# A transformer layer step on one core: halved border tiles leave PSUM by halves, the fourth tile starts on half of the tokens, and the last sums of squares stand behind three operands

## The reference, cut to what matters

```
h  = x + 0.5 * rmsnorm(swiglu(rmsnorm(x, g1), Wg, Wu, Wd), g1post)        # feed-forward 1
p  = rmsnorm(h, gmix) @ W_in         # gates and forget gate, fox q k v, nsa q k v
o  = concat(rmsnorm(fox_attention(p)), rmsnorm(nsa_attention(p)))
h2 = h + rmsnorm(o @ W_out, gmixpost)
y  = h2 + 0.5 * rmsnorm(swiglu(rmsnorm(h2, g2), Wg2, Wu2, Wd2), g2post)    # feed-forward 2
```

## Time and profile before

| | |
|---|---|
| median of three runs | 1217.18 us (1216.4 to 1220.91) |
| time of the profiled execution | 1218.23 us |
| its span | 1216.1 us |
| TensorE busy, share of the span | 96% |
| VectorE, ScalarE, GpSimd | 45%, 35%, 12% |
| mean granted TensorE clock | 0.983 |
| DMA | 117.53 MB, mean 97 GB/s |
| border a | about 400 to 441 us from the span's start |
| border b | about 805 to 845 us |

### The profile page before, as it was taken

One profiled execution on the slowest core, in us unless ns is written; L12 is line 12 of the kernel. 1 busy time (PEld: TensorE's weight loads), 2 busy tenths in 40 slices (PEclk: granted clock), 3 DMA queues, 4 the chain that ended last, 5 costly groups with the idle time before them and its releaser, 6 DMA issues.

```text
span 1216.1 us, 23337 instructions
## 1 busy us (share of the span) xinstructions
PE 1165.3 (96%) x9450; PEld 1076.8 (89%) x9460; DVE 542.6 (45%) x845; ACT 426.5 (35%) x779; POOL 146.4 (12%) x151
## 2 busy tenths in 40 slices
PE   8999999999999989998998899989999999999996
PEld 6999999999999889996545556978999999999995
DVE  3443333334333844354545767584333323343335
ACT  5322221222234642223523546464222212232332
POOL 0101100001012000131301312200011000010110
PEclk9999999999999999998998999999999999999998
DMA  6313222322123124224754310311232233232232
GB/s 277 105 69 103 81 85 83 113 92 103 58 87 120 50 90 157 88 70 120 162 144 143 105 70 2 121 53 63 77 103 81 68 102 100 101 104 69 67 105 73
DMA packets 50321, 117.53 MB, mean 97 GB/s; under 512 B 8347, under 2 KB 27163, under 8 KB 44579
## 3 DMA queue, kind: packets, MB, share of 16 engines
q1 hardware_dynamic: 48210, 112.68, 28.3%
q10 hardware_dynamic: 2032, 3.74, 0.8%
HBM read 107.79 MB, written 7.97 MB: 95 GB/s over the span
## 4 chain that ended last, share of the span: by engine, by line
PE 89%; DVE 5%; issue 3%; ACT 2%; DMA 1%; SPq 0%; DVEq 0%; ACTq 0%
PE ps L1627 69%; PE ps L1673 4%; PE ps L2123 3%; PE ps L1827 2%; PE ps L1860 2%; PE ps L1844 2%; PE ps L1894 1%; DVE row_max L1295 1%; DVE PTS L534 1%; DVE Y L1119 1%; PE ps L1636 1%; PE ps L1701 1%; DMA RAW<-in_w_gu 1%; PE ps L1835 1%; PE ps L1790 1%
## 5 line engine op out<-in xcount | busy, mean ns | idle before, releaser
L1627 PE MATMUL ps<-XH,WH 128*128 128x260 f32 x1680 | 342.3, 285 | 8.4 <-DVE XL L1081 3.3
L463 ACT CAST WH<-RAW 128x1024 fp32r<-128x1024 f32 (+2 forms) x177 | 168.7, 953 | 509.4 <-PE ps L1627 496.8
L1627 PE MATMUL ps<-XH,WL 128*128 128x260 f32 x1680 | 339.6, 284 | 0.0
L1627 PE MATMUL ps<-XL,WH 128*128 128x260 f32 x1680 | 339.1, 284 | 0.0
L1627 PEld LDWEIGHTS ps<-XH,WH 128*128 128x128 f32 x1680 | 261.0, 189 | 10.9 <-issue 8.3
L466 DVE TENSOR_TENSOR WL<-RAW,WH 128x1024 fp32r<-128x1024 f32 (+2 forms) x177 | 196.5, 1110 | 153.4 <-ACT WH L463 152.1
L1627 PEld LDWEIGHTS ps<-XH,WL 128*128 128x128 f32 x1680 | 260.2, 189 | 0.0
L1627 PEld LDWEIGHTS ps<-XL,WH 128*128 128x128 f32 x1680 | 259.5, 189 | 0.0
L1532 POOL TENSOR_TENSOR UL<-HT,UH 128x520 f32 (+1 forms) x44 | 57.7, 1311 | 634.1 <-ACT UH L813 634.1
L1627 PE MATMUL ps<-UL,WH 128*128 128x260 f32 x664 | 133.8, 283 | 0.0
L1627 PE MATMUL ps<-UH,WL 128*128 128x260 f32 x664 | 133.5, 282 | 0.0
(11 more groups left out here) (292 smaller groups left out, 1291.0 us busy)
## 6 DMA issues: line engine op xcount, KB each, us to landing
RAW<-in_w_gu SPq DMA_DIRECT2D x43, 1024.0 KB, 4.8
RAW<-in_w_down SPq DMA_DIRECT2D x16, 768.0 KB, 4.6
RAW<-in_w_down SPq DMA_DIRECT2D x16, 640.0 KB, 4.3
RAW<-in_w_in SPq DMA_DIRECT2D x10, 1024.0 KB, 4.9
KF<-in_fox_k SPq DMA_DIRECT2D x16, 256.0 KB, 4.2
VF<-in_fox_v SPq DMA_DIRECT2D x16, 256.0 KB, 4.0
RAW<-in_w_out SPq DMA_DIRECT2D x4, 1024.0 KB, 5.6
H<-in_x SPq DMA_DIRECT2D x4, 520.0 KB, 7.8
```

The lines of the kernel that those rows point to most:

```text
L463: nc.scalar.copy(hi[:, 0:width], RAW[:, slot, j, 0:width]).then_inc(w_hi, 1)
L1627: q = nc.tensor.matmul(ps[:, 2 * slot + half, 0:HALF], w[:, par, cols], x[:, kt0 + kt, half * HALF:(half + 1) * HALF], start=first and kt ...
```

## The change

1. `half_sums(s, 1)` (for a and b) moves from ahead of the warm-up into `border_products`, behind the third operand of half 0. TensorE waits for all three early items behind the warm-up.
2. VectorE copies each of the three tiles out in two halves: half 0 after half 0's 1/rms (`halves_out`), half 1 after half 1's. `first_halves` counts the three tiles whose half 0 is complete.
3. TensorE does the fourth item in two halves (`fourth_half`): half 0 straight behind the border, in bank 2, whose content is then copied out already; half 1 after the second half of that tile is out. At a the transposes of the first tile stand between them.
4. ScalarE's and VectorE's split of the fourth item, and ScalarE's scale of half 0, move from amid the operands to behind them. At a, the split of the fifth item moves there too, from `project`.
5. The logarithm of these scales is written into another buffer (`SQ`).
6. `softplus` loads one table set that has both its functions.

```diff
                 e = 1 if factor == 4 else 0
-                nc.scalar.activation(ST[:, 0, columns(h)], ps[:, 4 + h, 0:HALF], ACT.Ln, scale=factor / D_MODEL,
+                log = (SQ if kind == "hss" else ST)[:, 0, columns(h)]
+                nc.scalar.activation(log, ps[:, 4 + h, 0:HALF], ACT.Ln, scale=factor / D_MODEL,
                                      bias=const("eps")[:, e:e + 1]).then_inc(sem(kind + "_ln"), 1)
                 act.wait_ge(sem(kind + "_ln"), since(kind + "_ln", s, h + 1))
-                nc.scalar.activation(dst[:, columns(h)], ST[:, 0, columns(h)], ACT.Exp, scale=-0.5).then_inc(
-                    sem(done), 1)
+                nc.scalar.activation(dst[:, columns(h)], log, ACT.Exp, scale=-0.5).then_inc(sem(done), 1)
...
                             half_rstd(s, 1, "yss", factor, GT[:, 0, :], "yrstd")
-                        elif h == 1 and t == 3:
-                            split(first + 3)
-                        elif h == 1 and t == 5:
-                            half_rstd(s, 0, "hss", 1, R1[:, :], "rstd")
+                split(first + 3)
+                half_rstd(s, 0, "hss", 1, R1[:, :], "rstd")
                 half_rstd(s, 1, "hss", 1, R1[:, :], "rstd")
+                if s == "a":
+                    split(first + 4)
...
+                nc.scalar.preload_act_table_set("natural_log_exp_and_others")
                 act.wait_ge(sem("lf_abs"), 1)
...
                 for j in range(NPROJ):
-                    if 2 <= j < NPROJ - 2:
+                    if 2 < j < NPROJ - 2:
                         split(IT_PROJ + j + 2)
...
                                                            op1=ALU.subtract).then_inc(sem("xlo"), 1)
-                        if h == 1 and t == 7 and name:
-                            split(first + 3)
                     if name:
...
                         nc.vector.tensor_tensor(Y[:, 4, c], Y[:, 4, c], Y[:, 5, c], ALU.add).then_inc(sem("hacc"), 1)
-                if name:
-                    dve.wait_ge(sem("rstd"), since("rstd", s, 2))
+                if not name:
+                    return
+                out = [TR[:, 0, :], TR[:, 1, :], TR[:, 2, :]] if s == "a" else [GT[:, 0, :], UT[:, 0, :], GT[:, 1, :]]
+                dve.wait_ge(sem("first_halves"), 3 if s == "a" else 6)
+                dve.wait_ge(sem("rstd"), since("rstd", s, 1))
+                for n in (1, 0, 2):
+                    nc.vector.tensor_tensor(out[n][:, columns(0)], ps[:, 2 * (0, 1, 3)[n], 0:HALF], R1[:, columns(0)],
+                                            ALU.mult).then_inc(sem("halves_out"), 1)
+                    if n == 1:
+                        split(first + 3)
+                dve.wait_ge(sem("rstd"), since("rstd", s, 2))
+                for n in range(3):
+                    dve.wait_ge(used, first + n + 1)
+                    nc.vector.tensor_tensor(out[n][:, columns(1)], ps[:, 2 * (0, 1, 3)[n] + 1, 0:HALF],
+                                            R1[:, columns(1)], ALU.mult).then_inc(sem("projected" if s == "a" else "evac"), 1)
+                if s == "a":
+                    split(first + 4)
...
                     if st.kind == "gu":
-                        dve.wait_ge(used, k + 1)
-                        nc.vector.tensor_tensor(two(GT[:, st.par, :]), halves(3 if f == 1 and st.number == 1 and st.g == 0
-                                                                              else 0), two(R1[:, :]),
-                                                ALU.mult).then_inc(sem("evac"), 1)
+                        known = st.number if f == 1 and st.g == 0 else None
+                        if known not in (0, 1):
+                            dve.wait_ge(used, k + 1)
+                            nc.vector.tensor_tensor(two(GT[:, st.par, :]), halves(0), two(R1[:, :]),
+                                                    ALU.mult).then_inc(sem("evac"), 1)
                         split_behind(f, st, 0)
-                        dve.wait_ge(used, k + 2)
-                        nc.vector.tensor_tensor(two(UT[:, st.par, :]), halves(1), two(R1[:, :]),
-                                                ALU.mult).then_inc(sem("evac"), 1)
+                        if known != 0:
+                            dve.wait_ge(used, k + 2)
+                            nc.vector.tensor_tensor(two(UT[:, st.par, :]), halves(1), two(R1[:, :]),
+                                                    ALU.mult).then_inc(sem("evac"), 1)
                         split_behind(f, st, 1)
...
                 for j in range(NPROJ + 1):
-                    if j < NPROJ:
+                    if 3 <= j < NPROJ:
                         dve.wait_ge(used, IT_PROJ + j + 1)
...
                                 dve.wait_ge(sem("turned_out"), 1)
-                        nc.vector.tensor_tensor(two(TR[:, j % 4, :]), halves(3 if j == 2 else j % 2), two(R1[:, :]),
+                        nc.vector.tensor_tensor(two(TR[:, j % 4, :]), halves(j % 2), two(R1[:, :]),
                                                 ALU.mult).then_inc(sem("projected"), 1)
-                    if j == 2:
-                        split(IT_PROJ + j + 2)
                     if j > 0 and TILES[j - 1] in ROPED:
...
-                for n in range(2):
-                    ready(first + n)
                 if s == "a":
...
                 keep_warm(WARM[1], 0)
-                ready(first + 2)
+                for n in range(3):
+                    ready(first + n)
                 for h in (0, 1):
...
                             q = part(n, kt, h)
-                            if h == 1 and kt == KT - 1:
+                            if h == 0 and kt == KT - 1:
+                                q.then_inc(sem("first_halves"), 1)
+                            elif kt == KT - 1:
                                 q.then_inc(used, 1)
+                        if h == 0 and kt == 2:
+                            half_sums(s, 1)
                         if kt >= KT - HSQ_PE:
...
+            def fourth_half(k, h):
+
+                par = k % 2
+                for kt in range(KT):
+                    q = half_product(WH[:, par, :], WL[:, par, :], kt, True, kt, 2 + h, h, kt == 0, kt == KT - 1)
+                if h == 1:
+                    q.then_inc(used, 1)
+
             def half_token_squares(s, h):
...
                         ready(k + 1)
+                        pe.wait_ge(sem("halves_out"), 4)
+                        fourth_half(k + 1, 0)
                         pe.wait_ge(sem("evac"), since("evac", f, st.M * 2))
-                        products((IT_F[f] + 1) % 2, KT, XH, XL, 1)
+                        fourth_half(k + 1, 1)
                         return
...
                                 q.then_inc(sem("half_done"), 1)
-                        half_sums(s, 1)
+                        if s == "c":
+                            half_sums(s, 1)
                         return
...
                 border_products("a", IT_PROJ)
+                ready(IT_PROJ + 3)
+                pe.wait_ge(sem("halves_out"), 1)
+                fourth_half(IT_PROJ + 3, 0)
+                turn(0)
                 pe.wait_ge(sem("projected"), 2)
-                turn(0)
-                for j in range(3, NPROJ):
+                fourth_half(IT_PROJ + 3, 1)
+                for j in (1, 2):
+                    pe.wait_ge(sem("projected"), j + 1)
+                    turn(j)
+                for j in range(4, NPROJ):
                     ready(IT_PROJ + j)
...
                     products((IT_PROJ + j) % 2, KT, XH, XL, j % 2)
-                    if j == 3:
-                        pe.wait_ge(sem("projected"), 3)
-                        turn(1)
                     turn(j - 1)
...
             q.then_inc(used, 1)
-            half_sums("b", 1)
             ffn(1, "b", "c")
```

## The result

The changed kernel takes 1200.09 us (median of 4 runs, 1198.45 to 1202.06) against 1216.83 us for the kernel before (1216.4 to 1220.91); the ratio is 0.9856 with a 95% interval of 0.983 to 0.9882, that is 16.7 us or 1.4% faster. The prediction said 1200.0 us in a range of 1197.0 to 1204.5. The profiled execution took 1198.45 us, 1196.5 of it the span.

What follows compares the result with a forecast made beforehand. TensorE, busy 96% of the span, was taken as the bound, losing time to stops and half clock at borders. Gains of 11.0 (a) and 6.75 (b) sum to 17.75 us; from median 1217.18, with 0.6 held back: 1200.0 us, range 1197.0 to 1204.5.

Steps and rivals of the forecast that it cites:

- Start of the border: At both borders, tiles start just behind the first operand, no longer after the last sums: 402.85 at a, 808.72 at b.
- Length of the border, S minus the start of the tiles: From first tile to S, the border's last matmul pair of squares: about 22.2 us at both borders.
- The fourth tile and the fifth item at a: Behind border a, half the fourth tile replaces 2.49 us idle; the fifth item starts at 431.8, 9.3 us earlier.
- The clock: At border a, TensorE's idle times go and full clock is kept: 1.74 us more, 11.0 in all there.
- The sixth weight: Behind border a: cast at 434.5, done at 436.9, wanted by TensorE at 437.6; margin 0.7 us, no cost.
- Border b: Fifth item starts 6.75 us earlier, 1.77 of it clock, despite a new 1.1 us stall for its weight.
- 0.6 held back for handovers: In the forecast total: 0.6 us kept back for handovers taken as free, making 1199.4 into 1200.0 us.
- A new stretch of half clock in the borders: Rival, chance 0.11: new idle times at b bring half clock; one stretch costs 1.75 us: 1201.8, two 1203.5.
- ScalarE is not the bound at a: Rival, chance 0.06: table loads cost twice 1.28 us, sixth weight 1.9 late, stall at b 1.3 longer: 1203.2.
- The overlap works: Rival, chance 0.04: first-half copies come behind the border, the fourth tile waits; 2.5 us back at each border, 1205.
- The gain is not lost further on: Rival, chance 0.05: the attention stage, with stops of its own, loses part of the gain: 1206 to 1213 us.
- The projections did not stay at half clock: Rival, chance 0.02: TensorE, started earlier, stays at 1.2 GHz through the projections: 1229 us.

Runs made afterwards that it cites:

- same: The changed kernel run again with no edit, to see its noise: 1200.10 us, ratio 0.9862 to the kernel before.
- sums_first: Changed kernel with the last sums of squares put back ahead of the warm-up: 1206.81 us, ratio 0.9931 to the kernel before.
- three_tables: Changed kernel without the explicit table load in softplus, so three loads at border a in place of two: 1201.15 us, one run.
- no_warm: Changed kernel without the 8 warm-up matmuls ahead of each border: 1200.90 us, ratio 0.9872 to the kernel before.
- whole_fourth: Changed kernel, but TensorE begins the fourth item only when both halves of the first two tiles are out: 1202.54 us, ratio 0.9902 to before.
- only_sums: Kernel before with only the last sums of squares moved behind three operands: 1208.08 us, ratio 0.9930 to the kernel before.
- same_again: The changed kernel unaltered once more, in a later series: 1199.73 us, ratio 0.9875 to the kernel before.

## Why the prediction was right

*Start of the border.* The tiles were forecast to begin 0.54 us behind the start of the first operand's low part (402.85 and 808.72 on the time line of before); they begin 0.63 us behind it at both borders (403.04 - 402.41 at a).

*Length of the border, S minus the start of the tiles.* Predicted 22.25 and 22.2; measured 22.19 (425.23 - 403.04) and, in `same`, within 0.02 of it at both borders. The sums cost the 0.8 us that was forecast: without them, in `sums_first`, it is 21.4.

*The fourth tile and the fifth item at a.* Predicted at S + 6.7, measured 6.78. The gain up to the fifth item was forecast as 9.3 and is 9.18, counted from the first operand: 441.09 - 402.31 before, 432.01 - 402.41 after.

*The clock.* 1.74 us more at a: the part of the ledger has 10.89 for a forecast of 11.0. The prediction priced the half clock behind two stops alone. The falls in the warm-ups of before stood unnamed in the 5.2 us (4.2 at b) from first operand to tiles that lie in its rows, so the sum has them all the same. The granted clock is 1.00 throughout both borders, in this trace and in the two of the same kernel.

*The sixth weight.* The cast was forecast at 434.5 and starts at 434.48; it is done in time. `three_tables` shows how thin the margin is: one load more and the weight is 0.47 us late.

*Border b.* The fifth item was forecast with a stall of 1.1 us at S + 7.3 and has 1.27, at S + 7.65 (824.07 - 816.42 in `same`, whose records are complete there). VectorE's low part takes 1.43 us again, as in the earlier trace rows, where I had put the usual 1.23. So the gain to that item is 6.3 and not 6.75; the part of the ledger has 6.0, and where the other 0.3 went is open. The parts sum to 10.9 + 6.0 = 16.9 where 17.75 was forecast; the 0.6 held back for handovers happened to cover most of it. That the forecast met the median to 0.1 us is luck: the gain between medians was 16.7, 15.7 and 15.2 us in three series, and the forecast took 17.2 off a median of before that was itself 0.35 us higher than that of the final four runs.

*The rivals.* A new stretch of half clock in the borders did not come, and `no_warm` and `whole_fourth` show that it can at longer idle times (3.5 us, and 1.9 us against the 1.76 us that stayed without effect). The argument that both new idle times were shorter than any followed by a fall was too narrow, though: in the trace of before, 1.55 us of idle time ahead of a transpose at 562.62 has half clock behind it from 564.4 on. ScalarE is not the bound at a. The overlap works. The gain is not lost further on: the attention stage varies by 3 us by itself. The projections did not stay at half clock.

What the prediction missed was outside of the change: before's profiled execution had 2.7 us in the attention stage that after's did not have. Starting from the median of before and not from that execution took 1.05 us of it off; how much of it the median of before holds, no trace shows.

The order of the parts by worth, each measured by taking it out of the changed kernel: the fifth weight's split at a with the table load 7.5 us, the place of the sums 5.5 us, the fourth item by halves 4.4 us. Their sum of 17.4 is near 16.9, but they are not independent: each holds the clock falls behind the idle time that came back, 2.8 us in the first. Put into the kernel before by itself, the place of the sums brings 6.0 us.

## What to carry to other kernels

When an engine waits at a border for a scalar of the whole row, look for work that needs only half of it, and put the release of buffers in the same halves; here 2.9 us of matmuls fitted into 2.5 us of waiting. Then ask at once what is late next: the next item's weight stood in a chain of ScalarE's, and without its own move, 7.5 of the 16.9 us would have been given back. A trace of one execution holds chance terms as large as small changes; cut it into parts at rows that both kernels have, and compare part by part.

## What the runs showed of the hardware

Behind an idle time of TensorE the granted clock may be 0.50 for some microseconds. In the 14 traces, idle times of 1.8 us and less at a and b were never followed by it; of those of 1.9 to 2.7 us some were (1.91, 2.45, 2.68 and 2.71 us) and some were not (2.02, 2.32, 2.49 and 2.70 us); those of 3.5 and 4.7 us always were. The price was 1.7 us (behind the 2.71 us at a of the kernel before) to about 3 us (behind the 2.68 us of `only_sums`, where the item of 5.77 us took 8.75). The bound of 1.8 us holds for these two places alone. At the start of the attention stage, where TensorE is less busy, 1.54 us of idle time was followed by half clock in `same_again` and not in the changed kernel's first trace, and the 1.8 us near the end of the kernel was followed by it in every trace. At the start of the attention stage the same code was at 1.00 in some executions and at 0.83 over 20 us in others, and that part took 241.1 or 244.2 us.

A table load of ScalarE took 1.28 us each time, and the next activation started within 0.02 us of its end wherever it had no data to wait for.
